# Two half-width tiles by seven products in the MLP up projections of a two-block decoder

## The reference

```python
def rmsnorm(x, g, eps=NORM_EPS):
    xf = x.astype(jnp.float32)
    y = xf * lax.rsqrt(jnp.mean(xf * xf, axis=-1, keepdims=True) + eps)
    return (y * g.astype(jnp.float32)).astype(x.dtype)

def sq_relu_mlp(h, w_in, w_out):
    return jnp.square(jax.nn.relu(h @ w_in)) @ w_out
...
x = x + sq_relu_mlp(rmsnorm(x, mlp_norm_g[layer]), mlp_w_in[layer], mlp_w_out[layer])
```

## Time and profile before

| | |
|---|---|
| three runs, us | 2314.33, 2317.78, 2318.52 (median 2317.78) |
| profiled execution, first to last instruction, us | 2313.1 |
| TensorE busy | 2271.9 us, 98% |
| GpSimd busy | 1225.6 us, 53% |
| VectorE busy | 1188.8 us, 51% |
| ScalarE busy | 576.2 us, 25% |
| chain that ended last | TensorE 93%, VectorE 3% |
| TensorE clock granted | 0.999 of full speed |

### The profile page before, as it was taken

How to read it: one execution, slowest core, us unless ns; L and a number is a source line. 1 busy time by engine, 2 the same in 40 slices (tenths; PEclk the granted TensorE clock), 3 DMA queues, 4 the chain that set the end, 5 groups by cost and what they waited for, 6 DMA issues and landing times.

```text
span 2313.1 us, 41830 instructions
## 1 busy us (share of the span) xinstructions
PE 2271.9 (98%) x16906; PEld 1835.7 (79%) x16906; DVE 1188.8 (51%) x1497; ACT 576.2 (25%) x1183; POOL 1225.6 (53%) x810
## 2 busy tenths in 40 slices
PE   8999999999999999999999999999999999999999
PEld 6876888688888877677888888888877778888887
DVE  8797333853333363896633433474057667434333
ACT  5553433320011122353200101111025532111000
POOL 4111001266666665575666666666645456666665
PEclk9999999999999999999999999999999999999999
DMA  4220000232332222111233232223321113232222
GB/s 153 91 92 29 3 4 26 86 100 92 99 99 92 100 91 82 55 38 56 92 99 100 91 100 96 95 94 134 100 73 46 38 47 100 91 100 91 99 99 83
DMA packets 50447, 188.34 MB, mean 81 GB/s; under 512 B 5616, under 2 KB 5744, under 8 KB 49808
## 3 DMA queue, kind: packets, MB, share of 16 engines
q1 hardware_dynamic: 49824, 183.37, 23.8%
q10 hardware_dynamic: 496, 3.12, 0.4%
HBM read 184.30 MB, written 2.10 MB: 81 GB/s over the span
## 4 chain that ended last, share of the span: by engine, by line
PE 93%; DVE 3%; issue 1%; POOL 1%; ACT 1%; DMA 0%; DVEq 0%; SPq 0%; POOLq 0%; ACTq 0%
PE ps L658 25%; PE ps L660 25%; PE ps L659 25%; PE ps L1264 2%; PE ps L1279 2%; PE ps L866 2%; PE ps L876 1%; PE ps L1245 1%; PE ps L671 1%; PE ps L1246 1%; POOL wlo L485 1%; PE ps L874 1%; PE ps L848 1%; PE ps L768 0%; PE ps L690 0%
## 5 line engine op out<-in xcount | busy, mean ns | idle before, releaser
L485 POOL TENSOR_TENSOR wlo<-raw,whi 128x1024 fp32r<-128x1024 f32 (+1 forms) x323 | 749.5, 2320 | 44.7 <-DVE wlo L2340 20.3
L472 POOL TENSOR_SCALAR whi<-raw 128x1024 fp32r<-128x1024 f32 x330 | 359.6, 1090 | 704.1 <-PE ps L660 684.4
L658 PE MATMUL ps<-HH,whi 128*128 128x512 f32 x1312 | 522.4, 398 | 0.8 <-POOL wlo L485 0.7
L660 PE MATMUL ps<-HH,wlo 128*128 128x512 f32 x1312 | 511.8, 390 | 0.0
L659 PE MATMUL ps<-HL,whi 128*128 128x512 f32 x1312 | 511.3, 390 | 0.0
L658 PE MATMUL ps<-hidH,whi 128*128 128x512 f32 x768 | 298.8, 389 | 0.0
L659 PE MATMUL ps<-hidL,whi 128*128 128x512 f32 x768 | 298.8, 389 | 0.0
L660 PE MATMUL ps<-hidH,wlo 128*128 128x512 f32 x768 | 298.8, 389 | 0.0
L658 PEld LDWEIGHTS ps<-HH,whi 128*128 128x128 f32 x1312 | 246.7, 188 | 61.8 <-issue 10.3
L660 PEld LDWEIGHTS ps<-HH,wlo 128*128 128x128 f32 x1312 | 246.5, 188 | 52.0
L659 PEld LDWEIGHTS ps<-HL,whi 128*128 128x128 f32 x1312 | 246.9, 188 | 49.4 <-issue 1.2
(11 more groups left out here) (484 smaller groups left out, 3478.3 us busy)
## 6 DMA issues: line engine op xcount, KB each, us to landing
raw<-stream SPq DMA_DIRECT2D x336, 512.0 KB, 3.3
X<-xT SPq DMA_DIRECT2D x2, 1024.0 KB, 6.6
X<-xT SPq DMA_DIRECT2D x1, 2048.0 KB, 8.1
CW<-cmpw ACTq DMA_DIRECT2D x1, 2048.0 KB, 8.1
out<-X SPq DMA_DIRECT2D x4, 512.0 KB, 2.7
cst<-consts SPq DMA_DIRECT2D x1, 483.5 KB, 9.0
c2f<-consts ACTq DMA_DIRECT2D x1, 466.0 KB, 3.2
c2s<-consts ACTq DMA_DIRECT2D x1, 466.0 KB, 5.7
```

Source lines behind the costliest of these rows:

```text
L472: pool.tensor_scalar(hi, raw[:, j, :].rearrange("p (k m) -> p k m", k=DT), 1.0, 0.0, ALU.mult, ALU.add)\
L485: return pool.tensor_tensor(wlo[:, s, a:z, :], raw[:, j, a * P:z * P].rearrange("p (k m) -> p k m", k=z - a), whi[:, s, a:z, :].bitcast(F3 ...
L658: pe.matmul(acc, whi[:, s, k, :], hi, start=start, stop=False)
L660: return pe.matmul(acc, wlo[:, s, k, :], hi, start=False, stop=stop)
```

## The change

Groups 0 and 1 stay as they were. For groups 2 to 7 (the loop's) the four tiles of a group are made as two pairs. In a pair the weights of two tiles are the 2 x 2 matrix of quarters A11, A12 (tile 1, first and second half of the 1024 input channels), A21, A22 (tile 2), the input a 2 x 2 matrix of (half of the channels, half of the tokens). Seven products of 128 x 512 weights by 512 x 256 inputs take the place of eight (the Strassen scheme in Winograd's form). Each of the seven is 4 k-steps by three matmuls of 256 columns.

- **Input forms**, once per MLP: VectorE scales X by gain and `rstd` (8 `x_scaled`), makes 5 sums of 1024 elements per partition, ScalarE 7 high parts (BH), VectorE 7 low parts (BL), beside groups 0 and 1 and the first down.
- **Weight forms**, per pair: VectorE makes 4 sums of quarters (SW, 512 elements), ScalarE all 7 high parts (FH), VectorE the low parts of forms 0 and 1, GpSimd those of forms 2 to 6 (FL). GpSimd no longer splits these up blocks. There is one buffer per form, written again once its product in the pair before is done.
- **Outputs**: products 0 to 3 go to banks 0 to 3, products 4, 5 and 6 are added into banks 0, 2, 3. ScalarE copies product 0 aside before product 4 is added (`snapshot`); VectorE makes differences and sums (`difference`, `difference_and_third`, `fourth_quarter`, `second_quarter`, `third_quarter`, 256 elements each, one PSUM operand), ScalarE the relu of each quarter, then squares and hidH as before. `rstd` is in the input already.
- VectorE's adds of a down are spread: tiles 2 and 3 come after the weight sums of the next pair.

The diff, cut to its core:

```diff
+    FH = at("FH", [P, 7, 4, P], zone(4), F32R)
+    FL = at("FL", [P, 7, 4, P], zone(5), F32R)
...
+        FORMS = ["A11+A12", "A11+A12+A21", "A21", "A11+A12+A21+A22", "A12", "A11+A21", "A22"]
+        SUMMED = {0: 0, 1: 2, 3: 3, 5: 1}
+        SUMS_DONE = {0: 1, 1: 3, 3: 4, 5: 2}
...
 @block.gpsimd
+            def form_lows(m, i, r):
+                for p in range(2, 7):
+                    pool.wait_ge(*count("form_hi", 7 * pair_number(m, i, r) + p + 1))
+                    low = pool.tensor_tensor(FL[:, p, :, :], form_source(m, r, p), FH[:, p, :, :].bitcast(F32), ALU.subtract)
+                    low.then_inc(count("form_lo", 0)[0] if p < 5 else S("split_ready"), 1)
+                pool.sem_inc(S("hi_ready"), 2)
...
+                with pool.Fori(0, 3) as i:
+                    form_lows(m, i, 0)
+                    form_lows(m, i, 1)
+                    split_down(m, i, 16)
+                    form_lows(m, i, 2)
+                    form_lows(m, i, 3)
+                    split_down(m, i, 24)
...
 @block.tensor
+                def pair_up(i, r):
+                    Q, b = pair_number(m, i, r), pair_block(m, i, r)
+                    if r == 0:
+                        pe.wait_ge(S("rel"), 8 * m + 8)
+                    for p, (bank, start) in enumerate([(0, True), (1, True), (2, True), (3, True), (0, False), (2, False), (3, False)]):
+                        if r == 0:
+                            pe.wait_ge(*count("x_form_lo", 7 * m + p + 1))
+                        if p < 2:
+                            pe.wait_ge(*count("form_lo_v", 2 * Q + p + 1))
+                        elif p < 5:
+                            pe.wait_ge(*count("form_lo", 3 * Q + p - 1))
+                        else:
+                            pe.wait_ge(S("split_ready"), b + p - 4)
+                        pe.wait_ge(*[count("snap", 2 * Q), count("chain", 5 * Q - 4), count("chain", 5 * Q - 1), count("chain", 5 * Q),
+                                     count("snap", 2 * Q + 1), count("chain", 5 * Q + 2), count("chain", 5 * Q + 3)][p])
+                        acc = ps[:, bank, 0:TH]
+                        for k in range(4):
+                            pe.matmul(acc, FH[:, p, k, :], BH[p][:, k, :], start=start and k == 0, stop=False, skip_group_check=True)
+                            pe.matmul(acc, FH[:, p, k, :], BL[p][:, k, :], start=False, stop=False, skip_group_check=True)
+                            mm = pe.matmul(acc, FL[:, p, k, :], BH[p][:, k, :], start=False, stop=k == 3, skip_group_check=True)
+                        mm.then_inc(count("prod", 0)[0] if p < 5 else S("blk"), 1)
...
                 with pe.Fori(0, 3) as i:
-                    up(base + 12 + i * 16, i * 2 + 2)
+                    pair_up(i, 0)
+                    pair_up(i, 1)
                     down(base + 16 + i * 16, i * 2 + 1, 1)
-                    up(base + 20 + i * 16, i * 2 + 3)
+                    pair_up(i, 2)
+                    pair_up(i, 3)
                     down(base + 24 + i * 16, i * 2 + 2, 0)
...
 @block.scalar
+                def form_high(i, r, p):
+                    Q, b = pair_number(m, i, r), pair_block(m, i, r)
...
+                    if p in SUMS_DONE:
+                        act.wait_ge(*count("form_sum", 4 * Q + SUMS_DONE[p]))
+                    if p < 5:
+                        act.wait_ge(*count("prod", 5 * Q - 4 + p))
+                    else:
+                        act.wait_ge(S("blk"), b + p - 4 - (6 if r % 2 == 0 else 2))
+                    act.activation(FH[:, p, :, :], form_source(m, r, p), ACT.Copy).then_inc(count("form_hi", 0)[0], 1)
...
+                def first_quarter(i, r):
+                    act.wait_ge(*count("prod", 5 * pair_number(m, i, r) + 5))
+                    act.activation(zT[r % 2][0][:, 0:TH], ps[:, 0, 0:TH], ACT.Relu).then_inc(count("snap", 0)[0], 1)
...
+                def turn_of_pairs(i, r):
+                    n = r + 1
+                    for p in range(7):
+                        form_high(i, r, p)
+                    snapshot(i, r)
+                    for p in range(4):
+                        form_high(i, n, p)
+                    first_quarter(i, r)
+                    form_high(i, n, 4)
+                    second_quarter(i, r)
+                    form_high(i, n, 5)
+                    form_high(i, n, 6)
+                    second_tile(i, r)
+                    square(i, r, 0)
+                    snapshot(i, n)
+                    square(i, r, 1)
+                    hidden_high(i, r, 0)
+                    hidden_high(i, r, 1)
+                    first_quarter(i, n)
...
 @block.vector
+                def group_of_pairs(i, r):
+                    n = r + 1
+                    form_sum(i, n, 0)
+                    form_sum(i, n, 1)
+                    difference(i, r)
+                    difference_and_third(i, r)
+                    form_sum(i, n, 2)
+                    form_low(i, n, 0)
+                    fourth_quarter(i, r)
+                    form_low(i, n, 1)
+                    form_sum(i, n, 3)
+                    second_quarter(i, r)
+                    third_quarter(i, r)
+                    difference(i, n)
+                    hidden_low(i, r, 0)
+                    difference_and_third(i, n)
+                    hidden_low(i, r, 1)
+                    fourth_quarter(i, n)
+                    second_quarter(i, n)
+                    third_quarter(i, n)
...
                 with dve.Fori(0, 3) as i:
...
+                    for n in range(4):
+                        form_sum(i, 0, n)
+                    form_low(i, 0, 0)
+                    form_low(i, 0, 1)
+                    add(base + 8 + i * 16, tiles=[2, 3])
+                    group_of_pairs(i, 0)
+                    add(base + 16 + i * 16, tiles=[0])
+                    hidden_low(i, 1, 0)
+                    hidden_low(i, 1, 1)
+                    add(base + 16 + i * 16, tiles=[1])
...
```

More of the change, by code:

```diff
@@ L33 @@
 QT = T // P
+TH = T // 2
 C = 64
@@ L618, in _ @@
             pool.wait_ge(S("split_ready"), third + 1)
-            splits(third + 1, NBLK)
+            splits(third + 1, START["mlp2"] + 12)
+            mlp_splits(2)
+            splits(START["mlp2"] + 60, NBLK)
         MIXES = [2, 0, 3]
@@ new lines, in x_form_low, with form_sum @@
+                def x_form_low(p):
+                    src = XQ[1, 1] if p == 0 else XQ[2, 2] if p == 3 else BF[p][:, :, :]
+                    dve.wait_ge(*count("x_form_hi", 7 * m + p + 1))
+                    mark(dve.tensor_tensor(BL[p][:, :, :], src, BH[p][:, :, :].bitcast(F32), ALU.subtract), "x_form_lo")
+                def form_sum(i, r, n):
+                    Q, b = pair_number(m, i, r), pair_block(m, i, r)
+                    j, turn = (base + PAIR_AT[r] + (n > 0)) % RAW, (base + PAIR_AT[r] + (n > 0)) // RAW + 4 * i
+                    if n < 2:
+                        dve.wait_ge(S(f"raw_in{j}"), (turn + 1) * 16)
+                    if n == 0:
+                        dve.wait_ge(S("split_ready"), b - 6)
+                    if n >= 2:
+                        dve.wait_ge(*count("form_sum", 4 * Q + n - 1 + (n == 3)))
+                    first = pair_raw(m, r, 0, 0) if n < 2 else SW[:, r % 2, 0 if n == 2 else 2, :]
+                    second = pair_raw(m, r, 0, 1) if n == 0 else pair_raw(m, r, 1, 1 if n == 3 else 0)
+                    dve.tensor_tensor(SW[:, r % 2, n, :], first, second, ALU.add).then_inc(count("form_sum", 0)[0], 1)
@@ L2304, in squares, with add @@
                                               ALU.subtract).then_inc(S("hid"), 1)
-                def add(b, last=False):
-                    for j in range(4):
+                def add(b, last=False, tiles=range(4)):
+                    for j in tiles:
                         dve.wait_ge(S("blk"), b + j + 1)
@@ L2323, in mlp @@
                 squares(base + 4, 1, 1)
-                add(base + 8)
-                with dve.Fori(0, 3) as i:
[L2326 to L2329, removed]
+                add(base + 8, tiles=[0])
+                x_form_low(4)
+                x_form_low(5)
+                add(base + 8, tiles=[1])
+                x_form_low(6)
+                with dve.Fori(0, 3) as i:
+                    for n in range(4):
[8 more added lines that the diff above has]
+                    add(base + 16 + i * 16, tiles=[1])
+                    for n in range(4):
+                        form_sum(i, 2, n)
+                    form_low(i, 2, 0)
+                    form_low(i, 2, 1)
+                    add(base + 16 + i * 16, tiles=[2, 3])
+                    group_of_pairs(i, 2)
+                    add(base + 24 + i * 16, tiles=[0])
+                    hidden_low(i, 3, 0)
+                    hidden_low(i, 3, 1)
+                    add(base + 24 + i * 16, tiles=[1])
+                add(base + 56, tiles=[2, 3])
                 add(base + 60, last=True)
```

153 lines of the change are left out of this document (146 added, 7 removed).

## The result

The changed kernel takes 2329.35 us (median of 4 runs, 2325.84 to 2330.17) against 2318.15 for the kernel before on the same chip (2314.33 to 2319.9): a ratio of 1.0048, with a 95% interval of 1.0034 to 1.0061. It is slower by half a per cent; I had forecast 2295 and a range of 2280 to 2324. Timed again later, against the kernel before in the same session, it gave a ratio of 1.0031 (1.0019 to 1.0043).

What follows compares the result with a forecast made beforehand. TensorE's matmul pace was taken to bound the kernel. Terms: -25.9 + 1.5 + 1 + 1 = -22.4 us on the span of 2313.1, to 2290.7; with 4.7 from span to median, 2295 us, range 2280 to 2324.

Steps and rivals of the forecast that it cites:

- Pace of the pairs: TensorE in the MLP loops: 84 matmuls a pair at 0.121 us, 10.16 for 10.88, 25.9 us less over 36 pairs.
- rival 4: TensorE's pairs: the fixed 0.0134 us a matmul goes, pace 0.109, 62 us less, 2260 with the additions; chance 0.03.
- rival 3: TensorE's pairs: the weight load sets the pace, 0.128 us a matmul, 2317, no change; chance 0.08.
- Waits of TensorE's queue: Before each product, four or five waits instead of one to three, hidden by the queue's lead: 0 us.
- transfers: Weight blocks come in the same order, the first two down blocks landing far before GpSimd wants them: 0 us.
- The tight place: First to second pair of a group: first_quarter, behind the fourth weight sum and high 3, ends 0.3 us early; no wait.
- rival 1: Pair step: two more GpSimd lows in the fourth sum's way, TensorE waits 2.3 us a group; 2336 to 2359; chance 0.19.
- rival 2: One short TensorE wait in each group of pairs, 0.4 to 1.2 us, 14 us back, 2309; chance 0.20.
- Input forms: VectorE's 20.7 us per MLP, beside two ups and a down, costs 0.5 us an MLP, 1.5 in all.
- The first group of a loop: It finds GpSimd's lows 0.6 us later, so TensorE waits 0.3, 1 us in all.
- smaller misses: An allowance of 1 us for small losses elsewhere in the kernel.
- The 4.7 us from span to median: The median of the runs lay 4.7 us above the span; carried over, span 2290.7 becomes 2295.

Runs made afterwards that it cites:

- experiment 4: On top of experiment 2, ScalarE instead of GpSimd makes whi in blocks 4 to 11 of each MLP; 2298.75 us, ratio 0.991.
- experiment 6: Experiment 2's kernel with the edits of experiment 4 and experiment 5 together; 2298.54 us, ratio 0.9906.
- experiment 8: The changed kernel, its VectorE order kept, with ScalarE making whi of blocks 4 to 11 of each MLP; 2326.93 us, ratio 1.0043.
- experiment 7: The changed kernel with GpSimd's whi and wlo of each MLP's blocks 4 to 11 made 8 columns wide, not 1024; 2289.64 us.
- experiment 2: The changed kernel with VectorE's input-form work in groups 0 and 1 moved from ahead of each relu to behind it; 2326.44 us, ratio 1.0031.
- experiment 9: Experiment 6 with VectorE's low of input form 3 moved behind the add of the first down's tile 0; 2291.23 us, ratio 0.9883.
- experiment 5: On top of experiment 2, rstd is copied to PSUM and x_scaled reads it there, GpSimd left as it is; 2309.54 us, ratio 0.9954.
- experiment 1: The kernel before with the input forms' work added, read by nobody, and without the seven products; 2352.08 us, ratio 1.0146.
- experiment 10: Experiment 9 with ScalarE's first_quarter of the first pair ahead of form 3's high of the second; 2293.28 us, ratio 0.9885.

## Why the prediction failed, point by point

- **Pace of the pairs: right.** 0.120 us a matmul measured, 0.121 taken from the earlier trace rows; 36 pairs give -29.0, the forecast said -25.9. The 1 ns that I added for caution is the 3.0 us that I named for it. Of 0.109 and of the load as the limit (rivals 4 and 3) nothing is seen. The Trainium skill's N / 2.4 + 2.5 ns (TensorE: Matmul & The Clock Gate, Back-to-back issue gap), which by that section counts no weight load, does not hold for these streams with a load each: 0.109 by it, 0.120 in the trace.
- **Waits of TensorE's queue, transfers: right at 0.** None of the 36 pairs of the changed kernel shows a gap: from start to start no matmul is more than 0.16 us behind the one before.
- **The tight place: right to a tenth of a us, in all groups, but partly by luck.** In the pair that starts at 596.27 the fourth weight sum (603.35 + 1.78) ends 8.86 us in, `first_quarter` 9.87; forecast 8.9 and 9.8, due 10.16 (10.07 as measured). VectorE, then ScalarE:
```profile
603.35 1.78 DVE L2528 TENSOR_TENSOR SW<-SW,raw 128x512 f32<-128x512 f32 x1
605.10 0.42 DVE L2562 TENSOR_TENSOR relT<-ps,tmpA 128x256 f32<-128x256 f32 x1
```
```profile
605.24 0.63 ACT L1855 ACTIVATE FH<-SW 128x512 fp32r<-128x512 f32 x1 [2.08 <-DVE SW L2528]
605.77 0.37 ACT L1867 ACTIVATE relT<-ps 128x256 f32<-128x256 f32 x1
```
  The last meeting is as forecast, 1.18 us on the fourth sum for my 1.2. The first two are not: I had 0.4 and 1.2 for the first two sums, they cost 1.18 together, and VectorE then waits 0.41 for TensorE's third product, which was in no term. That product sets the date: the third sum ends 5.62 us in also where the first two end early (2.09 and 2.69 in the first group), and my 1.6 only happened to give the same.
  Rivals 1 and 2 were fair warnings of a place that did not decide; a wait there came only with ScalarE's `whi` (0.5 us in experiments 4, 6 and 8).
- **Input forms: the step that failed.** "Laid end to end they finish about 5 us before the first pair"; "I take 0.5 each", with ends 0 and 8. It is 11.5 an MLP, 34.6 in all for 1.5, and outside my ends. Three errors are in it; the runs price the second and the third, and the first only together with them:
  1. *The date.* I measured the work against the start of the first pair. What is due first in that queue is the add of tile 0, 10.9 us into the down, and VectorE begins its first relu only behind the reciprocal, at 492.87: 39.3 us and not "the 65 us of two ups and a down". Undisturbed, 26.3 of work and 9.0 of stops for ScalarE fit into them, by 3.2 us as experiment 7 shows; what is left for meetings is 3 us, and they took 12. The date that I did look at was never the tight one: in experiment 7 the last input form is done 8.3 us before the first pair, where I had about 5.
  2. *"GpSimd's whi, with one input, I take to hold nobody."* It holds VectorE's operations of two SBUF inputs just as `wlo` does (experiment 2's trace). GpSimd so shuts them out for 1.05 + 2.40 of every 5.44 us. Moving `whi` off GpSimd takes the wait from 8.3 to 0.8 (experiments 2 and 4), though only with the relu ahead of the forms (experiment 8). The earlier trace rows had been read for the `wlo` of the pair of lines alone; hidL there starts after `whi` has ended, and so could not tell.
  3. *What a late VectorE costs.* 9.0 us of idle time a down come with 2.3 more at the lower clock.
- **Other additions.** The first group of a loop: 1 us taken, 0 measured. The 1 us for smaller misses stands against 0.5 in the other downs; 4.5 in the hybrid stage and 2.8 ahead of the first MLP were in no term. The 4.7 us from span to median that I carried over is no fixed addition: in every run with both numbers the time is 1.7 to 2.2 us above the span (2.5 in experiment 7), and the rest is one execution against another.
- **The rivals.** None had the mechanism. The slower one was priced at 2336 to 2359 for a chain inside the pairs; the kernel is slower from a stretch ahead of them, on engines that the page shows at 51% and 53% busy.

Corrected for the failed term the sum stands to within 5 us: with nothing in the way of the forms, 2289.6 (experiment 7, one run, with part of the computation left out) and, as a complete kernel, 2291.2 (experiment 9), against my 2295.

## What to carry to other kernels

Work given to an engine that is half idle has to be laid into its queue up to the first thing due behind it, not up to the date of its own result: here an add, due 10.9 us into a down, before which VectorE used to sit idle for 4.16 us. Between VectorE and GpSimd, count the time that either holds the other off, one-input operations of GpSimd included, and add it up like a third engine. And when a cure on its own does nothing, look which wait stands there now: experiment 8's was another one, and with a change of order that also did nothing alone it was worth 28 us.

## What the hardware showed that I had not expected

- GpSimd's tensor_scalar with one SBUF input (1.05 us for 1024) and VectorE's operations with two exclude each other; both are recorded longer (1.38, 2.19 for 1.41). VectorE's operations with one operand in PSUM are not held: the relus stay at 0.68, the adds at 1.27 for two, also beside `wlo`.
- fp32r matmuls of 256 columns, each with its weight load, run at 0.120 us for 168 in a row at the upper clock.
- In one stage of the hybrid layer, which no edit touches, the same instructions take 21.6 us in the kernel before and in experiments 4 to 7, 23.1 to 24.6 in 1, 8, 9 and 10, and 26.1 in the changed kernel (both times) and experiment 2. Before and after:
```profile
1708.27:1729.90 21.63, 20.56 (x90) 14.44 (x87) 14.32 (x17) 8.36 (x21) 7.31 (x5) 1.00 0.18 51
```
```profile
1715.04:1741.17 26.13, 25.06 (x91) 16.86 (x87) 15.43 (x18) 11.08 (x25) 7.29 (x5) 0.80 0.17 58
```
  The granted clock makes the difference, 1.00 and 0.80. In all twelve traces TensorE stands idle for 1.07 us there until VectorE has written R; in some the clock falls behind it, in others it stays. What decides it is open: no run varied it by itself. It is up to 4.5 us, about the 0.2% that the measurement can tell, and it takes part in the comparison of any two kernels here.
